# One hybrid decoder layer on one core: gate and up of the feed-forward parts with seven products of sums in half of their blocks

## The chip, the core and the metric

The kernel runs on one core of a Trainium2 chip. The metric is the device time of one execution in microseconds, lower is better. The engines are TensorE (PE, its weight loads PEld), VectorE (DVE), ScalarE (ACT), GpSimd (POOL) and SyncE (SP), which issues most loads.

## The reference

The layer takes 256 tokens of width 2048. It has two feed-forward parts (FFN) of hidden width 5632, and between them a mixing part (attention and a recurrent group) that the change doesn't touch but for the form of one update.

```python
def swiglu(h, w_gate, w_up, w_down):
    return (jax.nn.silu(h @ w_gate) * (h @ w_up)) @ w_down
...
x = x + 0.5 * swiglu(rmsnorm(x, norm_ffn1[i]), w1_gate[i], w1_up[i], w1_down[i])
...
x = x + jnp.concatenate([o_mla, o_rwkv], axis=-1) @ w_out[i]
x = x + 0.5 * swiglu(rmsnorm(x, norm_ffn2[i]), w2_gate[i], w2_up[i], w2_down[i])
```

All tensors are float32.

## The kernel before

**Products.** Every float32 product is made of three matmuls of 128x128 by 128x512: each operand is split into a part in the fp32r type and a remainder (`hi`, `lo`), and hi x hi, hi x lo and lo x hi are added up in PSUM. The tokens are two tiles of 128 (TT = 2). Their transposed form for all 16 contraction tiles lies in `xT_hi` and `xT_lo` during an FFN; `gains` are multiplied in as it is made (`turn_x` on TensorE, `xT_parts_hi` on ScalarE, `xT_parts_lo` on VectorE).

**Blocks.** Weights come in blocks of 1 MB (128 partitions x 2048 columns). Block n goes through a ring: SyncE loads it into one of three buffers of `raw` (it waits until `split_lo` of block n - 3 is done, semaphore `lo_ready`), ScalarE copies it to `whi` (`split_hi`, three buffers, may run when block n - 3 has been used), VectorE takes the difference as `wlo` (`split_lo`, two buffers, when block n - 2 has been used, `block_used`), and TensorE uses it for 24 matmuls. Each engine has its queue in program order, and semaphores are the only ties between them.

**Passes.** The hidden width is 11 pieces of 512 columns (NFF = 11). One piece takes four gate blocks, four up blocks and four down blocks. The first piece has its gate and up blocks alone; then come ten passes (`pe_columns`, `dve_columns`, and the loop in `act_ffn`), nine in a hardware loop and one outside. In pass i TensorE does gate of piece i + 1 into banks 0 and 1, turns the hidden rows of piece i (`h_turn`, eight transposes into banks 6 and 7), does up of piece i + 1 into banks 2 and 3, and the four down blocks of piece i in banks 4 to 7. Beside it ScalarE makes `silu_g`, VectorE makes `hidden` after the last up block, the low part of the turned rows (`hT_part_lo`) and `update_x`, which adds half of a down chunk of 512 columns to x in two instructions, one for each token tile. A last `down` closes the FFN. ScalarE and VectorE run one block ahead of TensorE: while TensorE uses block n, VectorE splits block n + 1, and what else it does in that stretch stands in the code under the same step s.

**First piece.** In FFN 1 the norm's sums of squares (`square_x`), its factor (`factor`, and a power on GpSimd) and the turning of x lie beside the first eight blocks.

Of the kernel before, what the change touches and what calls it, by code (L numbers as in the profile page):

```python
# [56 lines left out]
BLOCKS = GATE + 16  # L57

# [59 lines left out]
def hybrid_layer(nc, table, w, out):  # L118
    where = constant_table()[1]
    ctx = ExitStack()  # L120
    with ctx:
# [150 lines left out]
        def sem(name):  # L272
# [13 lines left out]
            sem, ("silu_ready", "h_ready", "h_turned", "hT_hi_ready", "hT_ready"))  # L286
        vec, pool_chain, zero_row = sem("vec"), sem("pool_chain"), sem("zero_row")
# [36 lines left out]
        READ_FFN1, READ_OUT, READ_FFN2 = 2, 2 + 4 * NFF, 6 + 4 * NFF  # L324
# [8 lines left out]

        def split_hi(act, n, it=0):
            if n >= BLOCKS:
                return
            wd = block_width(n)
            act.wait_ge(raw_loaded[n % RAW], 16 * (n // RAW + 1) + 64 * it)
            if n >= WHI:
                act.wait_ge(block_used, n - WHI + 1 + 12 * it)  # L340
            nc.scalar.activation(whi[:, n % WHI, 0:wd], raw[:, n % RAW, 0:wd], ACT.Copy).then_inc(hi_ready, 1)  # L341

        def split_lo(dve, n, it=0):
            if n >= BLOCKS:
                return
            wd = block_width(n)
# [23 lines left out]
        def turn_bank(k, u):  # L370

            return 4 + u if k == 2 and u < 2 else 2 + (u % 6 if k == 0 else u % 2)

        def turn_x(pe, k, units):

            for u in units:
                if k == 0 and u % 2 == 0:
                    pe.wait_ge(x_loaded[u // 2], 16)
                if k and u % 2 == 0:
                    pe.wait_ge(banks_read, (READ_FFN1 + 4 * NFF, READ_FFN2, READ_FFN2 + 4 * NFF)[k - 1] - 3 + u // 2)  # L380
                if u >= {0: 6, 2: 4}.get(k, 2):
                    pe.wait_ge(xT_ready, 8 * k + u - (1 if k else 5))
# [32 lines left out]
        def h_turn(pe, f, i, it=0, b=6):  # L415
            pe.wait_ge(h_ready, NFF * f + i + 1 + it)
            if b == 6:
                pe.wait_ge(banks_read, (READ_FFN1, READ_FFN2)[f] + 4 * i + 4 * it)
# [6 lines left out]
        def down(pe, f, n, i, it=0, last=False, turn_next=False):  # L425
            h_hi, h_lo = (last_hT_hi, last_hT_lo) if last else (hT_hi, hT_lo)
            for j in range(4):
                if turn_next and j == 2:
                    h_turn(pe, f, i + 1, b=0)
                if j == 0:  # L430
                    pe.wait_ge(hT_ready, NFF * f + i + 1 + it)
                if j >= 2 or last:
                    pe.wait_ge(banks_read, (READ_FFN1, READ_FFN2)[f] + 4 * i + j - 1 + 4 * it)
                products(pe, n + j, h_hi, h_lo, range(FKT), [(4 + 2 * (j % 2), 5 + 2 * (j % 2))], COLS, True, True, it)
# [3 lines left out]
        def first_products(pe):  # L438

            for j in range(FKT):  # L440
                pe.wait_ge(first_lo_ready if j < FKT // 2 else lo_ready, 1)
                for t in range(TT):
                    acc, c = PS[:, t, :], slice(j * COLS, (j + 1) * COLS)
                    a, b = xT_hi[:, j, t * P:(t + 1) * P], xT_lo[:, j, t * P:(t + 1) * P]
                    nc.tensor.matmul(acc, a, whi[:, 0, c], start=j == 0, stop=False)
                    nc.tensor.matmul(acc, a, wlo[:, 0, c], start=False, stop=False)
                    ins = nc.tensor.matmul(acc, b, whi[:, 0, c], start=False, stop=False)
            ins.then_inc(block_used, 1)

        def pe_columns(pe, f, n, i, it=0, turn_next=False):  # L450

            pe.wait_ge(silu_ready, NFF * f + i + 1 + it)
            for s in range(4):
                products(pe, n + s, xT_hi, xT_lo, range(4 * s, 4 * s + 4), [(0, 1)], COLS, s == 0, s == 3, it)
            h_turn(pe, f, i, it)
            for s in range(4):
                products(pe, n + 4 + s, xT_hi, xT_lo, range(4 * s, 4 * s + 4), [(2, 3)], COLS, s == 0, s == 3, it)
            down(pe, f, n + 8, i, it, turn_next=turn_next)

        def pe_ffn(pe, f, B):  # L460
            turn_x(pe, 2 * f, range(2 * f, 4))
            for s in range(4):
                pe.wait_ge(xT_ready, 16 * f + 2 * s + 2)
                if (f, s) == (0, 0):
                    first_products(pe)
                else:
                    products(pe, B + s, xT_hi, xT_lo, range(4 * s, 4 * s + 4), [(0, 1)], COLS, s == 0, s == 3)
                if s < 2:
                    turn_x(pe, 2 * f, (2 * s + 4, 2 * s + 5))
            if f == 0:  # L470
                pe.wait_ge(banks_read, 1)
                pe.wait_ge(xT_ready, 6)
                pe.wait_ge(gains_loaded, 80)
                nc.tensor.transpose(PS[:, 7, 0:70], gain_rows[:, :], ident[0:70, 0:70]).then_inc(gains_turned, 1)
            for s in range(4):
# [1595 lines left out]
```

## Time and profile before

| what | value |
|---|---|
| median of 3 runs | 2046.76 us (2046.42 to 2051.57) |
| span of the profiled execution | 2045.4 us |
| TensorE's matmuls busy | 2017.3 us, 99% |
| VectorE busy | 1142.9 us, 56% |
| ScalarE busy | 869.0 us, 42% |
| granted clock of TensorE, mean | 0.999 |

The profiled execution has no time of its own in the results; its span runs from the first to the last instruction, and the median of the runs lies 1.4 us above it. Busy times of matmuls overlap in their pipeline, so a busy TensorE isn't a TensorE at its peak. A wait in a row is put down to the engine whose semaphore came last.

### The profile page before, as it was taken

To read this page: it belongs to the slowest core of one execution; us is meant where nothing else is said; L and a number is where in the kernel's file an instruction comes from. 1 tells how busy PE (TensorE), PEld (TensorE's weight loads), DVE (VectorE), ACT (ScalarE), POOL (GpSimd) and SP (SyncE) were. 2 spreads that over 40 slices of the span, in tenths; PEclk is the share of its full clock that TensorE was granted. 3 is DMA by queue.
4 is the path that set the end of the run, shared out by engine and by line. 5 is a ranking of instruction groups with operands and counts; after the bars stand their busy time and mean duration, and the time that the engine had idled before them with its cause. 6 is when DMAs were issued, how large, how long until landed. Compare 5 with 4: busy or idle time off the path is not lost.

```text
span 2045.4 us, 27608 instructions
## 1 busy us (share of the span) xinstructions
PE 2017.3 (99%) x11416; PEld 1683.9 (82%) x11416; DVE 1142.9 (56%) x1012; ACT 869.0 (42%) x847; POOL 134.9 (7%) x110
## 2 busy tenths in 40 slices
PE   8999999999999999999998999999999999999999
PEld 6888888888888889888787888888888888888887
DVE  4455545554555464756788545545554555545564
ACT  6333333333333345854344345333333333343353
POOL 0000000000000001344433000000000000000000
PEclk9999999999999999999999999999999999999999
DMA  7565555655655556667412556555656655555554
GB/s 262 186 195 195 185 185 191 198 185 187 195 193 185 191 155 215 201 196 221 123 41 70 190 165 206 185 186 194 193 185 190 195 189 187 193 195 185 186 185 144
DMA packets 190049, 373.62 MB, mean 183 GB/s; under 512 B 7110, under 2 KB 16962, under 8 KB 189980
## 3 DMA queue, kind: packets, MB, share of 16 engines
q1 hardware_dynamic: 186300, 361.47, 54.9%
q0 software_dynamic: 3680, 11.15, 1.8%
q8 instruction: 53, 0.87, 0.2%
q14 instruction: 16, 0.13, 0.0%
HBM read 363.94 MB, written 5.52 MB: 181 GB/s over the span
## 4 chain that ended last, share of the span: by engine, by line
PE 96%; DVE 2%; issue 0%; DMA 0%; ACT 0%; SPq 0%; DVEq 0%
PE PS L364 29%; PE PS L366 29%; PE PS L365 29%; PE PS L1341 3%; PE PS L421 1%; PE PS L385 1%; PE PS L1305 0%; DMA x_resid<-in_x 0%; DVE wlo L350 0%; DVE AB L1675 0%; PE PS L1412 0%; PE PS L1323 0%; PE PS L1279 0%; DVE AK L1675 0%; PE PS L1270 0%
## 5 line engine op out<-in xcount | busy, mean ns | idle before, releaser
L350 DVE TENSOR_TENSOR wlo<-raw,whi 128x2048 fp32r<-128x2048 f32 (+1 forms) x338 | 777.5, 2301 | 759.5 <-PE PS L366 755.5
L341 ACT ACTIVATE whi<-raw 128x2048 fp32r<-128x2048 f32 (+1 forms) x338 | 643.1, 1903 | 988.9 <-PE PS L366 983.9
L364 PE MATMUL PS<-whi,xT_hi 128*128 128x512 f32 (+2 forms) x1936 | 752.6, 389 | 0.0
L366 PE MATMUL PS<-whi,xT_lo 128*128 128x512 f32 (+2 forms) x1936 | 748.0, 386 | 0.0
L365 PE MATMUL PS<-wlo,xT_hi 128*128 128x512 f32 (+2 forms) x1936 | 747.5, 386 | 0.0
L366 PEld LDWEIGHTS PS<-whi,xT_lo 128*128 128x128 f32 x1936 | 363.5, 188 | 73.4
L364 PEld LDWEIGHTS PS<-whi,xT_hi 128*128 128x128 f32 x1936 | 363.6, 188 | 72.1 <-issue 0.4
L365 PEld LDWEIGHTS PS<-wlo,xT_hi 128*128 128x128 f32 x1936 | 363.7, 188 | 71.7
L364 PE MATMUL PS<-whi,hT_hi 128*128 128x512 f32 x680 | 264.8, 389 | 0.1
L366 PE MATMUL PS<-whi,hT_lo 128*128 128x512 f32 x680 | 264.6, 389 | 0.0
L365 PE MATMUL PS<-wlo,hT_hi 128*128 128x512 f32 x680 | 264.6, 389 | 0.0
L364 PEld LDWEIGHTS PS<-whi,hT_hi 128*128 128x128 f32 x680 | 127.6, 188 | 26.8 <-issue 0.5
L366 PEld LDWEIGHTS PS<-whi,hT_lo 128*128 128x128 f32 x680 | 127.6, 188 | 26.5
L365 PEld LDWEIGHTS PS<-wlo,hT_hi 128*128 128x128 f32 x680 | 127.6, 188 | 26.4
L556 DVE SCALAR_TENSOR_TENSOR x_resid<-PS,x_resid 128x512 f32<-128x512 f32 x184 | 118.0, 682 | 51.0 <-PE PS L366 51.0
L826 POOL TENSOR_TENSOR rstd<-rstd,con 128x2 f32<-128x2 f32 x6 | 6.3, 1044 | 1610.6 <-DVE rstd L821 1610.6
L403 DVE SCALAR_TENSOR_TENSOR xT_lo<-PS,gains,xT_hi 128x256 fp32r<-128x256 f32 x64 | 26.6, 477 | 28.1 <-ACT xT_hi L394 28.0
L394 ACT ACTIVATE xT_hi<-PS,gains 128x256 fp32r<-128x256 f32 x64 | 25.3, 476 | 38.0 <-PE PS L385 33.6
L1341 PE MATMUL PS<-XT,AB 64*64 64x64 f32 x640 | 26.4, 227 | 7.5 <-DVE XT L1689 4.8
L1341 PEld LDWEIGHTS PS<-XT,AB 64*64 64x64 f32 x640 | 22.1, 139 | 12.0 <-DVE XT L1702 5.7
L541 DVE SCALAR_TENSOR_TENSOR h<-PS,rstd,silu_g 128x512 f32<-128x512 f32 x44 | 30.9, 743 | 0.0
L547 DVE TENSOR_TENSOR hT_lo<-PS,hT_hi 128x1024 fp32r<-128x1024 f32 x20 | 24.5, 1224 | 10.1 <-ACT hT_hi L490 10.1
(334 smaller groups left out, 1079.6 us busy)
## 6 DMA issues: line engine op xcount, KB each, us to landing
raw<-in_w_gate SPq DMA_DIRECT2D x88, 1024.0 KB, 5.2
raw<-in_w_up SPq DMA_DIRECT2D x88, 1024.0 KB, 5.2
raw<-in_w_down SPq DMA_DIRECT2D x88, 1024.0 KB, 5.1
raw<-in_w_in SPq DMA_DIRECT2D x28, 1024.0 KB, 5.6
raw<-in_w_out SPq DMA_DIRECT2D x16, 1024.0 KB, 5.1
raw<-in_w_ple_gate SPq DMA_DIRECT2D x16, 1024.0 KB, 5.1
raw<-in_w_q_b SPq DMA_DIRECT2D x3, 1024.0 KB, 5.5
z_scratch<-zst POOLq DMA_DIRECT2D x6, 512.0 KB, 3.2
```

What stands on the lines that cost most here:

```text
L341: nc.scalar.activation(whi[:, n % WHI, 0:wd], raw[:, n % RAW, 0:wd], ACT.Copy).then_inc(hi_ready, 1)
L350: nc.vector.tensor_tensor(wlo[:, n % WLO, 0:wd], raw[:, n % RAW, 0:wd], f32(whi[:, n % WHI, 0:wd]), ALU.subtract).then_inc(lo_ready, 1)
L364: nc.tensor.matmul(acc, a, whi[:, n % WHI, c], start=st, stop=False)
L365: nc.tensor.matmul(acc, a, wlo[:, n % WLO, c], start=False, stop=False)
L366: ins = nc.tensor.matmul(acc, b, whi[:, n % WHI, c], start=False, stop=en)
L385: ins = nc.tensor.transpose(PS[:, turn_bank(k, u), j * SEQ + t * P:j * SEQ + (t + 1) * P], x[:, t, (2 * u + j) * P:(2 * u + j + 1) * P], i ...
L394: ins = nc.scalar.activation(xT_hi[:, kt, :], PS[:, turn_bank(k, u), j * SEQ:(j + 1) * SEQ], ACT.Copy, scale=gains[:, 16 * k + kt:16 * k + ...
L403: ins = nc.vector.scalar_tensor_tensor(xT_lo[:, kt, :], PS[:, turn_bank(k, u), j * SEQ:(j + 1) * SEQ], gains[:, 16 * k + kt:16 * k + kt + ...
L541: ins = nc.vector.scalar_tensor_tensor(h[:, t, :], PS[:, 2 + t, :], rstd[:, 4 * f + t:4 * f + t + 1], silu_g[:, t, :], ALU.mult, ALU.mult)
L547: nc.vector.tensor_tensor((dst or hT_lo)[:, :, :].rearrange("p (b j) s -> p b (j s)", b=2), PS[:, b:b + 2, :], f32((hi or hT_hi)[:, :, :]) ...
L556: ins = nc.vector.scalar_tensor_tensor(x[:, t, j * COLS:(j + 1) * COLS], PS[:, b + t, :], factor, x[:, t, j * COLS:(j + 1) * COLS], ALU.mu ...
L1341: ins = nc.tensor.matmul(PS[half(c), bank, out_col:out_col + CHUNK], a[half(c), s, a_cols], b[half(c)], start=start, stop=stop)
```

## The change

Take two contraction tiles (a pair) and both token tiles as a 2 x 2 block matrix A, and the pair's rows of the up and gate weights as a 2 x 2 block matrix B. Then A x B is the up and gate contribution of that pair for both token tiles. It takes eight products of blocks, or seven products of sums and differences of blocks with more additions (Winograd's form).

- A block now holds a pair with 512 columns of up and of gate (`load_unit`, two loads of 512 KB). Eight such units replace four gate and four up blocks.
- The first piece uses eight products for all pairs. In the ten passes, units 1, 3, 5 and 7 (pairs 0 to 3) use seven products, the even ones (pairs 4 to 7) eight.
- Weight sums: `weight_forms` (three dependent VectorE instructions on 1024, 512 and 512 columns into `T`), `forms_hi` (ScalarE, 2048), `forms_lo` (VectorE, 2048 into `t_lo`). Three quarters of the raw unit are split as before (1536 columns, `first_col`).
- Token sums: once for each FFN and each of four pairs, `token_sums` and `token_lo` on VectorE and `token_hi` on ScalarE, beside blocks 4 to 7 of the first piece. They overwrite the pair's part of `xT_hi` and `xT_lo` and fill `more_hi` and `more_lo`.
- The seven sums add up in PSUM banks over the four units; then `first_sum` (ScalarE) and `combine_gate`, `combine_up` (VectorE, five instructions) form gate and up. The even units add into banks 1, 4, 6 and 7.
- All eight PSUM banks are in use by the units. A pass now starts with `h_turn` into banks 2 and 3, then has the units of piece i + 1, then the down blocks, of which chunk j uses banks 2j and 2j + 1. `h_turn` waits for the `update_x` of chunk 2 of the pass before, the third output of the first unit for that of chunk 3.
- `hidden` is made under the down blocks. In the first piece it comes straight before `h_turn`.
- `update_x` is one instruction of 1024 columns, everywhere it is used.
- x is turned one unit of two tiles at a time after each block.

The diff, cut to its core:

```diff
+        def weight_forms(dve, n, it=0):
...
+            nc.vector.tensor_tensor(T[:, 0:2, :], src[:, 1:3, :], src[:, 0:1, :].broadcast_to([P, 2, COLS]),
+                                    ALU.subtract).then_inc(t_pair, 1)
+            dve.wait_ge(t_pair, forms_of(n, it))
+            nc.vector.tensor_tensor(T[:, 2, :], T[:, 1, :], src[:, 1, :], ALU.add).then_inc(t_third, 1)
+            dve.wait_ge(t_third, forms_of(n, it))
+            nc.vector.tensor_tensor(T[:, 3, :], T[:, 2, :], src[:, 3, :], ALU.subtract).then_inc(t_ready, 1)
...
+                ins = seven_product(m, P1, False, first, last)
+                if last:
+                    ins.then_inc(p_done, 1)
+                seven_product(m, P3, False, False, last)
+                seven_product(m, P2, False, False, last)
+                pe.wait_ge(t_lo_ready, forms_of(m, it))
+                if v == 1:
+                    pe.wait_ge(hT_ready, NFF * f + i + 1 + it)
+                for product in (P6, P7, P4):
...
-        def pe_columns(pe, f, n, i, it=0, turn_next=False):
...
+        def pe_pass(pe, f, i, it=0, turn_next=False):
+            if i:
+                pe.wait_ge(x_updated, evacs(f, i - 1, 2) + 4 * it)
+            h_turn(pe, f, i, it)
+            pe_units(pe, f, i, it)
+            down(pe, f, i, it, turn_next=turn_next)
...
-            for t in range(TT):
-                ins = nc.vector.scalar_tensor_tensor(x[:, t, j * COLS:(j + 1) * COLS], PS[:, b + t, :], factor,
-                                                     x[:, t, j * COLS:(j + 1) * COLS], ALU.mult, ALU.add)
-            ins.then_inc(banks_read, 1)
+            nc.vector.scalar_tensor_tensor(x[:, :, j * COLS:(j + 1) * COLS], PS[:, banks[0]:banks[1] + 1, :], factor,
+                                           x[:, :, j * COLS:(j + 1) * COLS], ALU.mult, ALU.add).then_inc(done, 1)
...
+        def dve_pass(dve, f, i, it=0, turn_next=False):
+
+            n = FFN_BASE[f] + PAIRS + 12 * i
             for s in range(12):
+                if s == 0 and i:
+                    down_out(dve, f, i - 1, 3, it)
+                if s == 8:
+                    combine_up(dve, f, i, it)
+                split_lo(dve, n + s + 1, it)
+                if s == 0:
                     hT_part_lo(dve, f, i, it)
+                if s in (0, 2, 4, 6):
+                    forms_lo(dve, n + s + 1, it)
+                if s in (1, 3, 5) or (s == 11 and not turn_next):
+                    weight_forms(dve, n + s + 2, it)
+                if s == 7:
+                    combine_gate(dve, f, i, it)
                 if s == 8:
+                    hidden(dve, f, i, it)
                 if s >= 9:
+                    down_out(dve, f, i, s - 9, it)
...
+            for s in range(PAIRS):
+                split_lo(dve, B + s + 1)
+                if s + 2 < PAIRS:
+                    xT_parts_lo(dve, 2 * f, (s + 2,))
+                if s >= 4:
+                    token_sums(dve, f, s - 4)
+                    token_lo(dve, f, s - 4)
...
+            weight_forms(dve, B + PAIRS + 1)
+            first_hidden(dve, f, B)
+            dve_pass(dve, f, 0)
```

The order of VectorE's instructions at the end of a pass, before: the last three down blocks, in the loop.

```order
L350 TENSOR_TENSOR wlo<-raw,whi 128x2048 [waits block_used,hi_ready]
L556 SCALAR_TENSOR_TENSOR x_resid<-PS,x_resid 128x512 [waits block_used]
L556 SCALAR_TENSOR_TENSOR x_resid<-PS,x_resid 128x512
L556 SCALAR_TENSOR_TENSOR x_resid<-PS,x_resid 128x512 [waits block_used]
L556 SCALAR_TENSOR_TENSOR x_resid<-PS,x_resid 128x512
```

The same place of the change (first of the ten passes; L425 is `split_lo`, L437 to L442 `weight_forms`, L782 `update_x`).

```order
L425 TENSOR_TENSOR wlo<-raw,whi 128x2048 [waits block_used,hi_ready]
L437 TENSOR_TENSOR T<-raw 128x1024 [waits raw_loaded0,t_lo_ready]
L440 TENSOR_TENSOR T<-T,raw 128x512 [waits t_pair]
L442 TENSOR_TENSOR T<-T,raw 128x512 [waits t_third]
L782 SCALAR_TENSOR_TENSOR x_resid<-PS,x_resid 128x2x512 [waits block_used]
```

The three sums of weights stand between the split and the update of chunk 2, for which TensorE's transposes now wait.

VectorE in the first piece before, around blocks 4 to 7 of FFN 1 (L821 is the norm's factor, L597 the copy of gains, L541 `hidden`).

```order
L350 TENSOR_TENSOR wlo<-raw,whi 128x2048 [waits block_used,hi_ready] x2
L821 TENSOR_SCALAR rstd<-sums 128x2 [waits squares]
L350 TENSOR_TENSOR wlo<-raw,whi 128x2048 [waits block_used,hi_ready] x3
L597 COPY gains<-PS 128x54 [waits gains_turned]
L350 TENSOR_TENSOR wlo<-raw,whi 128x2048 [waits block_used,hi_ready] x2
L541 SCALAR_TENSOR_TENSOR h<-PS,rstd,silu_g 128x512 [waits block_used,silu_ready]
```

The change at block 5 (L504 is `xT_parts_lo`, L792 to L800 `token_sums`, L804 and L806 `token_lo`).

```order
L504 SCALAR_TENSOR_TENSOR xT_lo<-PS,gains,xT_hi 128x256 [waits xT_hi_ready]
L504 SCALAR_TENSOR_TENSOR xT_lo<-PS,gains,xT_hi 128x256
L792 TENSOR_TENSOR tok<-xT_hi,xT_lo 128x2x2x128 [waits block_used]
L796 TENSOR_SCALAR tok<-tok 128x128 [waits vec]
L797 TENSOR_TENSOR tok<-tok 128x128
L798 SCALAR_TENSOR_TENSOR tok<-tok 128x128
L799 SCALAR_TENSOR_TENSOR tok<-tok 128x128 [waits vec]
L800 TENSOR_TENSOR tok<-tok 128x128 [waits vec]
L804 TENSOR_TENSOR xT_lo<-tok,xT_hi 128x512 [waits tok_hi]
L806 TENSOR_TENSOR more_lo<-tok,more_hi 128x384
L425 TENSOR_TENSOR wlo<-raw,whi 128x2048 [waits block_used,hi_ready]
```

A token step now stands ahead of each split from block 6 on, and holds a wait for ScalarE (`tok_hi`).

## Rows read from the trace of the kernel before

**Rows 1.** The page: span, and busy time of each engine

```profile
span 2045.4 us, 27608 instructions
...
PE 2017.3 (99%) x11416; PEld 1683.9 (82%) x11416; DVE 1142.9 (56%) x1012; ACT 869.0 (42%) x847; POOL 134.9 (7%) x110
```

**Rows 2.** The page: the chain that ended last, by engine

```profile
PE 96%; DVE 2%; issue 0%; DMA 0%; ACT 0%; SPq 0%; DVEq 0%
```

**Rows 3.** The chain in order of time, a pass: start us, us, what

```profile
147.72 0.87 PE PS L421 x8
...
213.91 0.87 PE PS L421 x8
```

**Rows 4.** Timeline of ScalarE in a pass: start, length, operation [idle before]

```profile
225.73 1.92 ACT L341 ACTIVATE whi<-raw 128x2048 fp32r<-128x2048 f32 x1 [3.52 <-PE PS L366]
231.17 1.92 ACT L341 ACTIVATE whi<-raw 128x2048 fp32r<-128x2048 f32 x1 [3.52 <-PE PS L366]
```

**Rows 5.** The page: groups of VectorE; xcount | busy us, mean ns | idle

```profile
L350 DVE TENSOR_TENSOR wlo<-raw,whi 128x2048 fp32r<-128x2048 f32 (+1 forms) x338 | 777.5, 2301 | 759.5 <-PE PS L366 755.5
...
L556 DVE SCALAR_TENSOR_TENSOR x_resid<-PS,x_resid 128x512 f32<-128x512 f32 x184 | 118.0, 682 | 51.0 <-PE PS L366 51.0
...
L547 DVE TENSOR_TENSOR hT_lo<-PS,hT_hi 128x1024 fp32r<-128x1024 f32 x20 | 24.5, 1224 | 10.1 <-ACT hT_hi L490 10.1
```

**Rows 6.** Timeline of VectorE in the same pass

```profile
236.68 2.29 DVE L350 TENSOR_TENSOR wlo<-raw,whi 128x2048 fp32r<-128x2048 f32 x1 [3.15 <-PE PS L366]
238.89 1.41 DVE L541 SCALAR_TENSOR_TENSOR h<-PS,rstd,silu_g 128x512 f32<-128x512 f32 x2
```

**Rows 7.** Groups of VectorE by form, columns as in rows 5

```profile
L350 DVE TENSOR_TENSOR wlo<-raw,whi 128x1280 fp32r<-128x1280 f32 x4 | 6.0, 1493 | 11.1 <-PE PS L366 11.1
...
L1067 DVE TENSOR_TENSOR sc<-sc,den 128x1024 f32<-128x1024 f32 x2 | 4.4, 2214 | 0.1
...
L1737 DVE TENSOR_TENSOR S<-PS,pc 128x128 f32<-128x128 f32 x4 | 1.2, 290 | 1.4 <-PE PS L1430 1.4
```

**Rows 8.** Timeline of VectorE near the end: each waits for the one before

```profile
2026.85 1.22 DVE L2029 TENSOR_TENSOR gate_s<-gate_s,proj 128x1024 f32<-128x1024 f32 x1
2028.10 1.23 DVE L2030 TENSOR_TENSOR x_resid<-x_resid,gate_s 128x1024 f32<-128x1024 f32 x1
```

**Rows 9.** Timeline of VectorE and TensorE where x is turned after FFN 1

```profile
746.76 1.66 DVE L403 SCALAR_TENSOR_TENSOR xT_lo<-PS,gains,xT_hi 128x256 fp32r<-128x256 f32 x4
...
747.79 1.35 PE L385 MATMUL PS<-con,x_resid 128*128 128x128 f32 x8 [1.50 <-DVE xT_lo L403]
```

**Rows 10.** Timeline of ScalarE in the first piece

```profile
31.37 1.92 ACT L410 ACTIVATE scratch<-x_resid 128x2048 f32<-128x2048 f32 x1
...
33.41 1.92 ACT L410 ACTIVATE scratch<-x_resid 128x2048 f32<-128x2048 f32 x1
...
39.89 1.28 ACT L485 ACT_TABLE_LOAD   x1
```

**Rows 11.** Windows at the end: length, busy (count) by engine, granted clock, DMA

```profile
2042.00:2043.50 1.50, 0.00 (x0) 0.00 (x0) 1.04 (x3) 0.00 (x0) 0.00 (x0) 0.79 0.22 76
2043.50:2045.40 1.90, 0.00 (x0) 0.00 (x0) 0.00 (x0) 0.00 (x0) 0.00 (x0) 0.50 0.23 78
```

**Rows 12.** Timeline of TensorE at the start

```profile
10.73 1.97 PE L385 MATMUL PS<-con,x_resid 128*128 128x128 f32 x8 [2.15 <-DMA x_resid<-in_x]
...
12.93 0.63 PE L446 MATMUL PS<-wlo,xT_hi 128*128 128x512 f32 x1
13.35 0.63 PE L447 MATMUL PS<-whi,xT_lo 128*128 128x512 f32 x1
...
19.34 1.04 PE L385 MATMUL PS<-con,x_resid 128*128 128x128 f32 x8
```

**Rows 13.** Timeline of ScalarE as FFN 2 begins

```profile
1219.23 2.07 ACT L1976 ACTIVATE proj<-PS 128x512 f32<-128x512 f32 x4 [1.61 <-PE PS L366]
```

**Rows 14.** The page: loads, KB each, us from issue to landing

```profile
raw<-in_w_gate SPq DMA_DIRECT2D x88, 1024.0 KB, 5.2
```

More of the change, by code:

```diff
@@ L423, in h_turn, with evacs, steps, eight_products @@
             ins.then_inc(h_turned, 1)
-        def down(pe, f, n, i, it=0, last=False, turn_next=False):
+        def evacs(f, i, j):
+            return 4 * ((NFF - 1) * f + i) + j + 1
+        def steps(f, i, k):
+            return 5 * ((NFF - 1) * f + i) + k
+        OUT_11, OUT_21, OUT_12, OUT_22 = (1, 0, 1), (4, 1, 1), (6, 0, 0), (7, 1, 0)
+        def eight_products(n, out, kk, first, last):
+            bank, t, side = out
+            kt, c = 2 * pair_of(n) + kk, slice((2 * kk + side) * COLS, (2 * kk + side + 1) * COLS)
+            a, b = xT_hi[:, kt, t * P:(t + 1) * P], xT_lo[:, kt, t * P:(t + 1) * P]
+            nc.tensor.matmul(PS[:, bank, :], a, whi[:, n % WHI, c], start=first, stop=False)
+            nc.tensor.matmul(PS[:, bank, :], a, wlo[:, n % WLO, c], start=False, stop=False)
+            return nc.tensor.matmul(PS[:, bank, :], b, whi[:, n % WHI, c], start=False, stop=last)
@@ new lines, in hybrid_layer, with token_form, seven_product @@
+        P1, P2, P3, P4, P5, P6, P7 = (0, 0, 1), (1, 1, 3), (6, 6, 2), (4, 2, 3), (5, 3, 0), (2, 4, 2), (3, 5, 1)
+        def token_form(f, p):
+            if f < 4:
+                return tuple(a[:, 2 * p + f // 2, (f % 2) * P:(f % 2 + 1) * P] for a in (xT_hi, xT_lo))
+            return tuple(a[:, p, (f - 4) * P:(f - 3) * P] for a in (more_hi, more_lo))
+        def seven_product(n, product, of_sums, first, last):
+            bank, f, k = product
+            a, b = token_form(f, pair_of(n))
+            c = slice(k * COLS, (k + 1) * COLS)
+            hi, lo = (t_hi[:, k, :], t_lo[:, k, :]) if of_sums else (whi[:, n % WHI, c], wlo[:, n % WLO, c])
+            nc.tensor.matmul(PS[:, bank, :], a, hi, start=first, stop=False)
+            nc.tensor.matmul(PS[:, bank, :], a, lo, start=False, stop=False)
+            return nc.tensor.matmul(PS[:, bank, :], b, hi, start=False, stop=last)
@@ L426, in down @@
+        def down(pe, f, i, it=0, last=False, turn_next=False):
+            n = FFN_BASE[f] + PAIRS + 12 * i + (0 if last else PAIRS)
             h_hi, h_lo = (last_hT_hi, last_hT_lo) if last else (hT_hi, hT_lo)
@@ L466, in pe_ffn @@
                 else:
[L467 to L475, printed above, removed]
-                products(pe, B + 4 + s, xT_hi, xT_lo, range(4 * s, 4 * s + 4), [(2, 3)], COLS, s == 0, s == 3)
@@ L477, in pe_ffn @@
-            with pe.Fori(0, NFF - 2) as it:
-                pe_columns(pe, f, B + 8, 0, it)
-            pe_columns(pe, f, B + FFN_BLOCKS - 16, NFF - 2, turn_next=True)
-            down(pe, f, B + FFN_BLOCKS - 4, NFF - 1, last=True)
-        def silu(act, f, B, it=0):
-            act.wait_ge(block_used, B + 4 + 12 * it)
+                    pe.wait_ge(lo_ready, B + s + 1)
+                    for out in (OUT_11, OUT_21, OUT_12, OUT_22):
+                        if (f, s) == (1, 0) and out == OUT_21:
+                            pe.wait_ge(proj_evac, 2)
+                        for kk in range(2):
+                            ins = eight_products(B + s, out, kk, s == 0 and kk == 0, s == PAIRS - 1 and kk == 1)
@@ L546, in hT_part_lo, with hidden @@
+        def hidden(dve, f, i, it):
+            dve.wait_ge(combined, steps(f, i, 5) + 5 * it)
+            dve.wait_ge(silu_ready, NFF * f + i + 2 + it)
+            for t in range(TT):
+                ins = nc.vector.scalar_tensor_tensor(h[:, t, :], h[:, t, :], rstd[:, 4 * f + t:4 * f + t + 1],
+                                                     G[:, 2 * t, :], ALU.mult, ALU.mult)
+            ins.then_inc(h_ready, 1)
+        def hT_part_lo(dve, f, i, it=0, dst=None, hi=None, b=2):
             dve.wait_ge(hT_hi_ready, NFF * f + i + 1 + it)
```

398 lines of the change are left out of this document (269 added, 129 removed).

## The prediction, made before the change was run

> **What bounds the kernel now.** The page comes first: TensorE is busy for 99% of the span VectorE for 56%, ScalarE for 42% [rows 1]. Busy shares alone don't name a bound, so the chain that ended last is next: 96% of it is TensorE's [rows 2]. In the feed-forward (FFN) loops the same chain shows the eight transposes of `h_turn` at 147.72 and 213.91 us [rows 3], so one pass is 66.19 us. The timeline of ScalarE has its copies 5.44 us apart, each after 3.52 us of waiting for TensorE [rows 4]. That is one weight block of 24 products: one product each 0.2267 us. Twelve blocks (288 products) are 65.3 us, and the transposes add 0.9 us. TensorE never waits inside a pass, and the others wait for it. VectorE spends some 35 us in a pass: twelve splits at 2.3, eight `update_x` halves at 0.68, two of `hidden` and `hT_part_lo` at 1.22 [rows 5].
>
> **The gain.** A unit of two row pairs holds the same two contraction tiles for gate and for up, so its eight 128x512 products (24 matmuls) can be seven (21). Four units per pass give 12 matmuls less. The first piece of each FFN keeps eight products, ten passes use seven: 2 x 10 x 12 = 240 matmuls, 240 x 0.2267 = **54.4 us less** work on TensorE. Nothing else in TensorE's streams changes in number but the grouping of transposes. A pass is then 276 x 0.2267 + 0.9 = 63.5 us if TensorE never waits.
>
> **What VectorE gets.** Prices are from rows: 2.29 us for 2048 columns, with the next unconnected instruction starting 2.21 after (236.68 to 238.89) [rows 6]; 1.22 for 1024 [rows 5]; 0.68 for 512 [rows 5]; for 1536 the 1280 form (1.49) and 2048 give 1.76; for 128 columns 0.29 [rows 7]. An instruction that waits for the one before it starts 0.03 after that one's end [rows 8], so a dependence costs 0.11 more than none. In a pass of seven products the splits cost 8 x 2.21 + 4 x 1.68 = 24.4; the sums of weights 4 x 2.6 = 10.4 and their low parts 4 x 2.21 = 8.8; the two combinations 1.26 + 0.73 + 0.61 + 1.26 + 1.15 = 5.0; `hidden` 1.3, `hT_part_lo` 1.15, four `update_x` of 1024 at 1.15 each 4.6, about 0.1 each under the two halves before. Together 55.7 us of 63.5, 88%. It fits as an average; what counts is where it doesn't fit.
>
> **End of each pass.** In the order now, the last down block is covered on VectorE by split, `weight_forms` and `update_x` of chunk 2, and TensorE's `h_turn` of the next pass waits for that `update_x`, since it writes banks 2 and 3 and the next unit bank 4. Before, `h_turn` stood four blocks into the pass with `hidden` done long ago. From the end of down block 2: 0.11 to VectorE's start, 2.21 split, 1.22 + 0.03 + 0.69 + 0.03 + 0.61 sums, 1.22 update (nearest row: 1.22 for 1024 columns out of PSUM) = 6.12, and 0.16 to TensorE's start. This last figure is from the turn of x, where a quarter of VectorE's group of four (1.66 us from 746.76) ends the wait for 747.79: the second instruction ends near 747.63 [rows 9], since each is 0.48 long and starts 0.39 after the one before. TensorE is ready 5.44 - 0.16 = 5.28 after the same end. The wait is 1.0, and inside the loop a register instruction stands in front of the transposes and holds this wait, so I take 1.1 (bounds 0.6, if the dependences cost nothing, and 1.5). Ten passes per FFN have nine such joints: 18 x 1.1 = **19.8**. Behind the waiting transposes stands the whole next unit. VectorE's queue then holds chunk 3's update, the split, `hT_part_lo` and the low parts: 1.15 + 1.68 + 1.15 + 2.29 = 6.3 us, and they are wanted only 0.9 + 5.4 + 2.0 = 8.3 us later, behind nine matmuls of the first seven-product unit. No stall there, nor at the other three (4.8 + 5.44 us of TensorE against 2.21 + 2.6 + 1.68 + 2.29 = 8.8).
>
> **Second down block.** `combine_gate` can start when product P6 of the last unit is done, 2.9 us into it, and ends 2.8 us later; then come 1.15 + 1.26 for `combine_up` and 2.21 for the split that down block 1 needs: 2.9 + 0.1 + 2.65 + 2.4 + 2.2 = 10.25 us against 4.76 + 5.44 = 10.2 of TensorE. With the 0.16 to start this is 0.25 per pass (0 to 0.6): 20 x 0.25 = **5.0**.
>
> **First piece.** Here `token_sums` and `token_lo` are new, four times per FFN, each with a trip over ScalarE in the middle while VectorE stands. One step: 0.69, four small ones in three dependences to 1.95 from its start, 0.05 to ScalarE, 1.05 for two copies, 0.05 back, 0.61 + 0.48: 4.2 us. Behind it in VectorE's queue is the split that TensorE needs next. After block 4: transposes, `xT_parts_hi` and `_lo` to 2.2 (0.48 each instruction [rows 9]), the step to 6.45, the split to 8.74, start 8.9, while TensorE is ready at 6.2: stall **2.7**. After block 5 `square_x` stands ahead of the token copy on ScalarE: two times 2.04 us [rows 10] behind a copy of 1.92 that ends at 9.1 on this clock, so the token step ends at 15.3 and the split at 17.6, and block 7 starts at 17.7 instead of 14.35: stall **3.4**. From there VectorE has two more steps (8.4), one split (2.2), the first `weight_forms` (2.6), `hidden` (1.4) and small ones (0.3), in all 15.1 us to the first `h_turn`, against 5.6 of block 7: stall **9.5**. ScalarE's table load of 1.28 [rows 10] and the silu end before `hidden` by this sum, so they cost nothing; without that cover they would cost about 1.3 after the last token copy, up to 1. Sum 15.6 per FFN (13 to 18, by 0.1 to 0.2 us per small instruction either way), **31.2** for two. Before, `hidden` had its turn under gate products.
>
> **The clock.** After nearly 10 us without a matmul I expect TensorE at its lower level. The trace shows it at the end: with no matmul after 2042, the granted clock is 0.79 up to 2043.5 and 0.50 from there on [rows 11], that is 1.2 of 2.4 GHz. At the start, after idle time, products follow 0.42 us apart instead of 0.23, and the granted clock isn't recorded low there, but the spacing says it [rows 12]. Seven products went so, 1.4 us lost, and eight transposes took 1.97 instead of 1.03 [rows 12]: **2.4** per event, two events: 4.8 (0 to 7). The stalls of 2.7 and 3.4 may lower it too, but the block behind each then runs under VectorE's longer chain. The Trainium skill ("TensorE: Matmul & The Clock Gate", section "HAM oscillation") says that idle gaps put TensorE back to half its clock and each has to be warmed up again; by that rule the penalty is in the sum, by a clock that stays up the time would be 2050. The trace agrees at its end.
>
> **Edges.** In FFN 1 eight transposes move behind the first product: 0.9 [rows 3]; an earlier first product could give some back, I take none. In FFN 2 the third product group waits for four copies of `proj`, 2.07 us from 1219.23 [rows 13], against 1.36 us of products: 1.1. Loads: two halves of 512 KB in place of 1 MB with the same three buffers; a block lands 5.2 us after its issue [rows 14], over 4 us ahead of its use by this schedule, so nothing. The copies `first_sum` and the silu on ScalarE lie beside TensorE; ScalarE has some 35 us of work in 64. Edges: **2.0**.
>
> **Sum.** -54.4 + 19.8 + 5.0 + 31.2 + 4.8 + 2.0 = +8.4. Against the profiled execution's span 2045.4 [rows 1] that is 2053.8; the median of the runs lies 1.4 above that span, so 2046.8 + 8.4 = **2055 us**.
>
> **Rivals.** (1) No change to speak of, chance 0.31: the waits come to 48 to 60 us. Clock at full level after the gap (-4.8) alone gives 2050; joints of 0.7 instead of 1.1 (-7.2) give 2048. For it: every term is a small difference of two long sums. Against: the first-pass chain is dependent work in queue order. (2) Faster, chance 0.13: the seven products pay because the token steps don't hold TensorE. The place is the three waits before the first `h_turn`; their price with the clock is 36 us, and without any of it the time is 2019. It decides below 21.5 us for both FFNs, 10.7 each. Only the last wait alone is 9.5 by rows. (3) Much slower, within the 0.56 for slower: the first sum reads one operand repeated over two halves. A VectorE row of the attention with a repeated operand took 2.21 us for 1024 columns, not 1.22 [rows 7]. At 1.0 more per joint and 2 in the first pieces this gives 2075; other repeated operands in this trace show no such cost, so 0.05 of the 0.56. Outside this, the forecast itself holds about 0.51.
>
> **How the numbers follow.** A measurement of this kernel tells about 0.3% (6.1 us) from no change; the bound for slower is 2052.9, 2 us under my sum. With all low bounds the sum is near -20, with all high ones +29; these don't come together, and some 12 us each way hold most: 2042 to 2066. The likeliest case alone is 2050 to 2062. Faster 0.13, same 0.31, slower 0.56.
>
> **What would show it.** In the changed profile: about 240 matmuls less; period of `h_turn` 64.8 to 65.0 us; TensorE waits for VectorE's update of x at each `h_turn` near 1 us, for the split before down block 1 near 0.3; three waits near 2.7, 3.4 and 9.5 us in each first piece, and slow products after the last. The prediction is wrong if the token steps overlap better, or if dependent VectorE instructions cost other than 0.03 after an end.

## The result and the profile after

The changed kernel takes 2063.14 us (median of 4, 2062.29 to 2063.84) against 2047.13 for the kernel before: ratio 1.0076, 95% interval 1.0062 to 1.0091. It is slower, as forecast, and inside the range of 2042 to 2066, near its upper end; but the sum said +8.4 and the profiled executions differ by 2061.8 - 2045.4 = 16.4 us.

The page after the change, against [rows 1, 5] (L782 is `update_x`):

```profile
span 2061.8 us, 28682 instructions
...
PE 1990.7 (97%) x11176; PEld 1643.4 (80%) x11176; DVE 1594.0 (77%) x1404; ACT 998.1 (48%) x963; POOL 137.9 (7%) x110
...
L782 DVE SCALAR_TENSOR_TENSOR x_resid<-PS,x_resid 128x1024 f32<-128x1024 f32 x92 | 110.5, 1218 | 19.7 <-PE PS L467 19.7
```

Matmuls fell by 240, to 11176. TensorE is busy for 97% of a longer span. Now the waits of TensorE, which decide (us in total, times, longest):

```profile
PE PS L520 <- DVE h L739: 16.4, 2, 8.8
PE PS L520 <- DVE x_resid L782: 14.6, 18, 0.8
PE PS L539 <- DVE wlo L425: 9.5, 4, 3.1
...
PE PS L539 <- ACT proj L2239: 0.8, 1, 0.8
```

L520 is `h_turn`, L539 the first product of a block. All the places that the sum names are there: two first `h_turn`s, 18 joints, four blocks of the first pieces, the third product group of FFN 2. The chain in order of time gives the stages (first pass and a steady one; last `h_turn` of FFN 1; the four transposes of p behind the mixing part; the same for FFN 2), to be laid beside [rows 3]:

```profile
75.22 1.94 PE PS L520 x8
...
142.82 1.09 PE PS L520 x8
...
207.92 1.09 PE PS L520 x8
...
663.54 1.09 PE PS L520 x8
...
717.00 0.87 PE PS L520 x8
...
1179.30 0.44 PE PS L2194 x4
...
1292.06 1.94 PE PS L520 x8
...
1358.84 1.10 PE PS L520 x8
...
1932.94 0.87 PE PS L520 x8
```

And the same marks in the chain of the kernel before (L421 is its `h_turn`, four blocks into the first pass, so 21.76 us behind the end of the first piece):

```profile
81.55 0.87 PE PS L421 x8
...
710.76 0.87 PE PS L421 x8
...
1168.81 0.44 PE PS L1931 x4
...
1287.22 0.87 PE PS L421 x8
...
1916.44 0.87 PE PS L421 x8
```

| stage | before | after | difference |
|---|---|---|---|
| start to end of first piece, FFN 1 | 59.79 | 75.22 | +15.4 |
| passes to the last `h_turn` | 650.97 | 641.78 | -9.2 |
| to the transposes of p (mixing) | 458.05 | 462.30 | +4.3 |
| to end of first piece, FFN 2 | 96.65 | 112.76 | +16.1 |
| passes to the last `h_turn` | 650.98 | 640.88 | -10.1 |
| rest | 128.96 | 128.86 | -0.1 |

Two things don't stand in the sum. The steady pass is 65.10 us long, over the 64.8 to 65.0 forecast, and the mixing part, in which no line is changed, is 4.3 us longer. The experiments follow them, and test the terms.

### The profile page after: what moved, and what is told of

It reads as the page before. It is cut to its first block, busy times and chain, and to the rows that moved or that the text cites. A ratio compares the mean times of both kernels' runs of the same rounds, so it can differ in the third digit from the quotient of the medians.

```text
span 2061.8 us, 28682 instructions
## 1 busy us (share of the span) xinstructions
PE 1990.7 (97%) x11176; PEld 1643.4 (80%) x11176; DVE 1594.0 (77%) x1404; ACT 998.1 (48%) x963; POOL 137.9 (7%) x110
## 4 chain that ended last, share of the span: by engine, by line
PE 88%; DVE 6%; issue 4%; ACT 1%; DMA 0%; DVEq 0%; SPq 0%
PE PS L465 12%; PE PS L467 12%; PE PS L466 12%; PE PS L539 8%; PE PS L541 8%; PE PS L540 8%; PE PS L557 6%; PE PS L556 6%; PE PS L558 6%; PE PS L1604 2%; PE PS L520 1%; DVE T L437 1%; DVE x_resid L782 1%; DVE wlo L425 1%; DVE T L440 1%
## 5 line engine op out<-in xcount | busy, mean ns | idle before, releaser
L425 DVE TENSOR_TENSOR wlo<-raw,whi 128x2048 fp32r<-128x2048 f32 (+2 forms) x338 | 732.2, 2167 | 295.9 <-PE PS L467 211.6
L416 ACT ACTIVATE whi<-raw 128x2048 fp32r<-128x2048 f32 (+2 forms) x338 | 606.4, 1795 | 417.1 <-PE PS L467 325.7
L539 PE MATMUL PS<-whi,xT_hi 128*128 128x512 f32 x768 | 307.1, 400 | 13.6 <-DVE wlo L425 9.5
L541 PE MATMUL PS<-whi,xT_lo 128*128 128x512 f32 x768 | 302.8, 394 | 0.0
L540 PE MATMUL PS<-wlo,xT_hi 128*128 128x512 f32 x768 | 301.6, 393 | 0.0
L465 PE MATMUL PS<-whi,xT_hi 128*128 128x512 f32 (+2 forms) x536 | 206.4, 385 | 0.0
L467 PE MATMUL PS<-whi,xT_lo 128*128 128x512 f32 (+2 forms) x536 | 203.6, 380 | 0.0
L466 PE MATMUL PS<-wlo,xT_hi 128*128 128x512 f32 (+2 forms) x536 | 203.4, 379 | 0.0
L539 PEld LDWEIGHTS PS<-whi,xT_hi 128*128 128x128 f32 x768 | 146.3, 191 | 45.6 <-issue 14.3
L541 PEld LDWEIGHTS PS<-whi,xT_lo 128*128 128x128 f32 x768 | 145.8, 190 | 32.7
L540 PEld LDWEIGHTS PS<-wlo,xT_hi 128*128 128x128 f32 x768 | 146.4, 191 | 30.8
L782 DVE SCALAR_TENSOR_TENSOR x_resid<-PS,x_resid 128x1024 f32<-128x1024 f32 x92 | 110.5, 1218 | 19.7 <-PE PS L467 19.7
L1089 POOL TENSOR_TENSOR rstd<-rstd,con 128x2 f32<-128x2 f32 x6 | 10.2, 1700 | 1614.3 <-DVE rstd L1084 1614.3
```

What stands on the lines that cost most here:

```text
L416: nc.scalar.activation(whi[:, n % WHI, a:wd], raw[:, n % RAW, a:wd], ACT.Copy).then_inc(hi_ready, 1)
L425: nc.vector.tensor_tensor(wlo[:, n % WLO, a:wd], raw[:, n % RAW, a:wd], f32(whi[:, n % WHI, a:wd]), ALU.subtract).then_inc(lo_ready, 1)
L465: nc.tensor.matmul(acc, a, whi[:, n % WHI, c], start=st, stop=False)
L466: nc.tensor.matmul(acc, a, wlo[:, n % WLO, c], start=False, stop=False)
L467: ins = nc.tensor.matmul(acc, b, whi[:, n % WHI, c], start=False, stop=en)
L539: nc.tensor.matmul(PS[:, bank, :], a, whi[:, n % WHI, c], start=first, stop=False)
```

## The experiments

"The kernel before" is timed beside each; it had 2046.85 to 2047.12. Times are medians.

**e_update: the other part of the change alone**, made in the kernel before.

```
-            for t in range(TT):
-                ins = nc.vector.scalar_tensor_tensor(x[:, t, ...], PS[:, b + t, :], factor, x[:, t, ...], ...)
-            ins.then_inc(banks_read, 1)
+            nc.vector.scalar_tensor_tensor(x[:, :, ...], PS[:, b:b + 2, :], factor, x[:, :, ...], ...).then_inc(banks_read, 1)
```

> The kernel before, with one part of the change alone: x is updated by one VectorE instruction over both token tiles in place of two. My theory: VectorE's update was never waited for there, so the time stays within 2 us of the kernel before (2047); an update of 1024 columns takes 1.22 us where the two halves took 1.29 together. Rival, that this part costs or gains time by itself (the next down block is waiting for the banks): then the time moves by more than 3 us either way, since it is done 88 times.

Measured: 2047.87 us, ratio 1.0005 (0.9995 to 1.0014). No cost of this part shows (the interval runs from -1.0 to +2.9 us), so most of the loss of 16 us lies with the seven products and their order.

**e_joint: the sums of weights behind the update that is waited for.**

```
-                if s in (1, 3, 5) or (s == 11 and not turn_next):
+                if s in (1, 3, 5):
                     weight_forms(dve, n + s + 2, it)
...
                     down_out(dve, f, i, s - 9, it)
+                if s == 11 and not turn_next:
+                    weight_forms(dve, n + s + 2, it)
```

> The changed kernel, with the sums of weights for the next pass's second unit (the call of weight_forms in the twelfth step of a pass) moved behind the update of chunk 2 that h_turn waits for. My theory, that the joint is a matter of VectorE's queue order: the wait at h_turn goes and nothing takes its place, the period falls from 65.10 to 63.7 to 64.0 us, and the time by 18 times 1.1 to 1.3 us, to 2040 to 2043. Rival, that VectorE is too full for the pass (55.7 us of work by the sum in 63.5): then the stall comes back at the next wait of TensorE, for the second unit's low parts or for chunk 3, the period stays above 64.7 and the time above 2056.

Measured: 2043.79 us, 0.9984 (0.9974 to 0.9993) of the kernel before: 19.4 less than the changed kernel. First VectorE at a joint of the changed kernel, and TensorE's `h_turn` there:

```profile
266.87 2.29 DVE L425 TENSOR_TENSOR wlo<-raw,whi 128x2048 fp32r<-128x2048 f32 x1 [2.01 <-PE PS L467]
269.08 1.22 DVE L437 TENSOR_TENSOR T<-raw 128x1024 f32<-128x1024 f32 x1
270.33 0.69 DVE L440 TENSOR_TENSOR T<-T,raw 128x512 f32<-128x512 f32 x1
271.06 0.69 DVE L442 TENSOR_TENSOR T<-T,raw 128x512 f32<-128x512 f32 x1
271.67 2.35 DVE L782 SCALAR_TENSOR_TENSOR x_resid<-PS,x_resid 128x1024 f32<-128x1024 f32 x2
...
273.02 1.09 PE L520 MATMUL PS<-con,h 128*128 128x128 f32 x8 [0.82 <-DVE x_resid L782]
```

The update starts 4.80 us after the split and `h_turn` stands until its first instruction ends. After the edit the update follows the split, and the chain has the transposes 64.03 us apart, (462.63 - 206.51) / 4, at their 0.87 us:

```profile
206.51 0.87 PE PS L520 x8
...
462.63 0.87 PE PS L520 x8
```

65.10 - 64.03 = 1.07 per joint, and no new wait of TensorE in the passes. The trace shows 0.82 of idle time, counted from the end of the matmul ahead. Without a wait `h_turn` starts before that end, which the same place after the edit shows:

```profile
270.13 0.40 PE L467 MATMUL PS<-whi,hT_lo 128*128 128x512 f32 x1
270.36 1.04 PE L520 MATMUL PS<-con,h 128*128 128x128 f32 x8
```

This overlap of 0.17 us (270.13 + 0.40 - 270.36) is lost with the wait, and makes up most of the other 0.25. The rival of a full VectorE falls.

**e_first: the first piece in another order.** The core, on VectorE:

```
                 split_lo(dve, B + s + 1)
+                if 2 <= s <= 5:
+                    token_lo(dve, f, s - 2)
+                if 1 <= s <= 4:
+                    token_sums(dve, f, s - 1)
                 if s + 2 < PAIRS:
                     xT_parts_lo(dve, 2 * f, (s + 2,))
-                if s >= 4:
-                    token_sums(dve, f, s - 4)
-                    token_lo(dve, f, s - 4)
```

ScalarE has `token_hi` at s of 1 to 4, a square each at 5 and 6, VectorE has the norm's `factor` one step later, and ScalarE's first silu waits for a new semaphore behind product group OUT_21 of block 7.

> The changed kernel with the first piece of each FFN put in another order: the token step of a pair is begun after blocks 0 to 3 of the first piece instead of 4 to 7, its last part (token_lo) stands one step later so that VectorE does not wait for ScalarE's copies, the two squares stand apart, and the first silu waits for the gate products of the last block alone. The work is the same. My theory (dependent work in queue order): the three waits of 2.4, 3.1 and 8.8 us in each FFN come down to about 3.3 in all, so 22 to 25 us go for two FFNs, and some 5 us of slow clock with them if the clock stays up: 2033 to 2041. Rival, that these waits are VectorE's amount of work and not its order: under 10 us go, 2053 or more. The clock is told apart by the granted clock over the first pass: with a wait of 3 us or less it stays at 1.0, or it falls all the same, and then 5 us less are won.

Measured: 2038.27 us, 0.9958 (0.9941 to 0.9974), 24.9 less than the changed kernel with the same work: already faster than the kernel before. What the step looked like in the changed kernel, VectorE and ScalarE after block 4:

```profile
45.10 0.68 DVE L792 TENSOR_TENSOR tok<-xT_hi,xT_lo 128x512 f32<-128x512 f32 x1
...
46.80 0.29 DVE L800 TENSOR_TENSOR tok<-tok 128x128 f32<-128x128 f32 x1
47.13 0.63 ACT L685 ACTIVATE xT_hi<-tok 128x512 fp32r<-128x512 f32 x1 [1.05 <-DVE tok L800]
47.67 0.51 ACT L686 ACTIVATE more_hi<-tok 128x384 fp32r<-128x384 f32 x1
48.21 0.69 DVE L804 TENSOR_TENSOR xT_lo<-tok,xT_hi 128x512 fp32r<-128x512 f32 x1 [1.11 <-ACT more_hi L686]
48.82 0.55 DVE L806 TENSOR_TENSOR more_lo<-tok,more_hi 128x384 fp32r<-128x384 f32 x1
49.29 2.28 DVE L425 TENSOR_TENSOR wlo<-raw,whi 128x2048 fp32r<-128x2048 f32 x1
```

4.19 us from its start to the split, 1.11 of it idle, as summed (4.2). In the new order the only waits left in the first pieces were those before the first `h_turn`s, 3.0 and 3.2 us, beside the start and the 0.8 for proj. Both answers to the question about the clock came: in FFN 1 the granted clock was 0.72 over the 6 us behind the wait of 3.0 us and the first pass took 66.74 us, 1.6 over the others; in FFN 2, after 3.2 us, it stayed at 1.00 and the pass took 65.13.

**e_all: both, and the split for down block 1 ahead of `combine_up`.**

```
-                if s == 8:
-                    combine_up(dve, f, i, it)
                 split_lo(dve, n + s + 1, it)
+                if s == 8:
+                    combine_up(dve, f, i, it)
```

> Both edits of the two other runs of the changed kernel together, and in each pass the split for the second down block ahead of combine_up. My theory: the terms add up. From 2063: 18 joints of 1.1 to 1.3 (20 to 23), 20 second down blocks of 0.25 (5), first pieces 22 to 25, clock 0 to 9, so 2002 to 2016, which is 1.5 to 2.2% under the kernel before, near what 240 matmuls are worth. Rival, that the seven products lose by VectorE being the bound: then the time stays near or over the kernel before, 2040 or more.

Measured: 2015.36 us, 0.9842 (0.9826 to 0.9859), in the range's upper end. The period is now (449.26 - 193.80) / 4 = 63.87:

```profile
193.80 0.87 PE PS L520 x8
...
449.26 0.87 PE PS L520 x8
```

So the early split is worth 64.03 - 63.87 = 0.16 per pass. In the changed kernel this wait shows in TensorE's weight loads for the down blocks (us in total, times, longest), and it is gone from e_all:

```profile
PEld PS L465 <- DVE wlo L425: 4.6, 16, 0.3
```

Nothing waits in this pass any more (TensorE is busy for all of it), and still it is longer than 276 x 0.2267 + 0.87 = 63.44. The 0.43 us that are left lie in the products themselves. Three runs looked for them, the first two made in the kernel of e_all.

**e_operands: where TensorE reads.**

```
-            hi, lo = (t_hi[:, k, :], t_lo[:, k, :]) if of_sums else (whi[:, n % WHI, c], wlo[:, n % WLO, c])
+            if of_sums:
+                c = slice((k % 3) * COLS, (k % 3 + 1) * COLS)
+            hi, lo = whi[:, n % WHI, c], wlo[:, n % WLO, c]
```

> Four of the seven products of a unit read sums of weights (tiles t_hi and t_lo); here they read columns of the block's own split (whi and wlo) instead, everything else as in the kernel with both edits and the early split, so the output is not the layer's. It asks where 0.43 us of each pass come from: the pass takes 63.87 us there, and 276 products at 0.2267 and the transposes make 63.44. Theory one, that the two more tiles which TensorE reads from cost it something: the period falls to 63.4 to 63.5 and the time by 8 us. Theory two, that it lies in what the other engines do or in TensorE's own stream: the period stays within 0.1 of 63.87 and the time within 2 us of 2015.

Measured: period 63.55, so 0.32 of the 0.43 gone. The time is 2009.47 us, but from two executions that lie 6.8 us apart (2006.07 and 2012.88); the period is the evidence.

**e_small_sums: less work for the neighbours.** The slices of T, t_hi and t_lo in `weight_forms`, `forms_hi` and `forms_lo` get `0:e`:

```
+            e = COLS if n in (FFN1 + PAIRS + 1, FFN2 + PAIRS + 1) else 8
```

> The same kernel with all its instructions, but the sums of weights and their two parts are made in full for the first unit of each FFN alone; after that they cover 8 of each 512 columns, so the products of sums read old values, and the output is not the layer's. VectorE has some 17 us less to do in each pass, ScalarE 7. Theory one, that work of the neighbours on the same memories slows the products: the period falls from 63.87 to about 63.45 and the time by about 8 us. Theory two, that it lies in TensorE's own stream: no change beyond 0.1 per pass. It is also the bound for this design: what is left above 2007 is then not VectorE's sums.

Measured: 2016.31 us, period 63.87 as before, though VectorE's busy time fell from 1590.6 to 1263.8 us. So it is not contention with the sums, and in this order VectorE's 327 us of them cost TensorE nothing; the splits and updates stayed, and were not tested. In e_operands the slow groups left were mostly those of more_hi (10 of 12 in a pass took 0.69 us). What t_hi, t_lo, more_hi and more_lo have in common is where they begin: 64 bytes past a multiple of 128 in each partition, by the sizes of the tiles ahead of them; whi, wlo, xT_hi and xT_lo begin at multiples.

**e_align: the changed kernel with this alone.**

```
+        base[0] += -base[0] % 128
         R0 = base[0]
```

> The changed kernel, nothing moved in any engine's order: all tiles from G on (t_hi, t_lo, more_hi, more_lo, h among them) lie 64 bytes further in each partition, so that they begin at multiples of 128 bytes, as whi, wlo, xT_hi and xT_lo do. Now they begin 64 bytes past one. Theory one, from the run in which products of sums read whi and wlo and the pass fell by 0.32 us with the products of more_hi still 0.69 us in three: TensorE reads slower from a place that is not a multiple of 128 bytes; then the period of h_turn falls from 65.10 by up to 0.43 us (65.10 less 0.35 to 0.45), 20 passes give 7 to 9 us, and the time is 2054 to 2056. Theory two, that it is the values or the distance of the tiles from the others: no change beyond 1 us, 2062 to 2064.

Measured: 2056.80 us, 6.3 under the changed kernel's 2063.14, and 1.0053 (1.0038 to 1.0068) of the kernel before; period (660.76 - 142.62) / 8 = 64.77, 0.33 less. Theory one holds, though both figures are a little short of it. The trace says why: this kernel still has the split for down block 1 in its old place, and the same wait for it has grown from 4.6 us:

```profile
PEld PS L466 <- DVE wlo L426: 6.0, 16, 0.4
```

These 1.4 us more are 0.07 for each of the 20 passes, which is what 0.33 lacks to the 0.40 found below where nothing waits.

Products at the end of a seven-product unit, TensorE's timeline, the first matmul of three successive groups, before the edit:

```profile
228.06 0.40 PE L556 MATMUL PS<-t_hi,xT_hi 128*128 128x512 f32 x1
...
228.76 0.39 PE L556 MATMUL PS<-t_hi,xT_hi 128*128 128x512 f32 x1
...
229.46 0.39 PE L539 MATMUL PS<-whi,xT_hi 128*128 128x512 f32 x1
```

and after it:

```profile
227.38 0.39 PE L557 MATMUL PS<-t_hi,xT_hi 128*128 128x512 f32 x1
...
228.06 0.39 PE L557 MATMUL PS<-t_hi,xT_hi 128*128 128x512 f32 x1
...
228.74 0.39 PE L540 MATMUL PS<-whi,xT_hi 128*128 128x512 f32 x1
```

A group of three matmuls took 0.70 us and now takes 0.68. The next block's first groups took 0.69 (229.46 to 230.15), though these read well-placed tiles in both, and are at 0.68 too.

**e_again: the changed kernel once more.**

> The changed kernel once more, for the clock in the mixing part. In its first profile the granted clock fell to 0.75 for some 10 us near 1125 us, and about 4 of the 16 us that the change lost lie there, though nothing of it stands there. Theory one, chance of the moment: in a second execution the clock falls elsewhere or not at all, and the last x-turn of the mixing part stands nearer 8 than 10 us behind the kernel before. Theory two, it belongs to this program's order in time: the same place and the same loss within 0.5 us, and the time within 1 us of 2063.

Measured: 2064.02 us. The second theory: the mixing part had 462.6 us against 462.3, with the clock low in the same place. The windows of the first and of the second execution (length, busy by engine, granted clock, DMA):

```profile
1100.00:1140.00 40.00, 35.18 (x626) 30.66 (x627) 29.19 (x63) 13.36 (x26) 12.21 (x8) 0.87 0.29 92
```

```profile
1100.00:1140.00 40.00, 34.78 (x624) 30.19 (x625) 29.38 (x64) 13.37 (x26) 12.20 (x8) 0.87 0.28 89
```

In its four stretches of 10 us the granted clock was 0.83, 1.00, 0.75 and 0.91 in the first execution, and 0.83, 1.00, 0.78 and 0.88 in the second; in the kernel before it was 1.00 from 1070 to 1130 us. The loss lies there too: from the last `h_turn` to the last products with `lora_t` in the chain (1080.23, before 1074.66) the changed kernel took 363.2 us against 363.9, and from there to the transposes of p 99.1 against 94.2.

But it is no property of the seven products alone: in the profile of e_update, all eight products, the same stretch took 1174.48 - 710.22 = 464.3 us, in an execution with a span of 2051.0 where the nine others had 2045.4 to 2047.5, and its granted clock fell to 0.67 and 0.78 between 1000 and 1020. In the profiles of all versions of the changed kernel the stretch took 461.0 to 464.2, with falls at several places.

**e_best, e_best2, e_best3: the rest of the wait before the first `h_turn`**, in the kernel of e_all. First on ScalarE and by token tile (the squares one block earlier, a small silu to load the table, the silu before the split), of which the part on VectorE is:

```
             for t in range(TT):
+                if t:
+                    dve.wait_ge(block_used, B + PAIRS)
+                else:
+                    dve.wait_ge(first_gate, 2 * f + 2)
```

> The kernel with both edits and the early split, and what is left of the wait ahead of the first h_turn (3.0 us in each FFN) taken down: the squares stand one block earlier, a small silu behind them brings ScalarE's table load into idle time, the first silu stands ahead of the next split, and hidden's first token tile starts when its three product groups of the last block are done and not at the end of the block. My theory: hidden's second tile alone stands behind the block, 0.7 us and the hand-overs, so the wait falls from 3.0 to 0.9 to 1.2 us, the clock stays up (1.6 us in FFN 1), and the time falls by 4 to 6 us to 2009 to 2011. Rival, that the wait has another last cause, VectorE's weight_forms or the squares: the wait stays above 2.5 us and the time within 1 us of 2015.

Measured: 2017.42 us, the waits 3.3 and 3.4: no gain. The rival had it, and the timeline of ScalarE and VectorE names the cause:

```profile
57.62 1.27 ACT L664 ACTIVATE G<-PS,rstd 128x512 f32<-128x512 f32 x2 [0.53 <-PE PS L541]
...
59.46 1.22 DVE L437 TENSOR_TENSOR T<-raw 128x1024 f32<-128x1024 f32 x1
...
61.44 0.69 DVE L442 TENSOR_TENSOR T<-T,raw 128x512 f32<-128x512 f32 x1
62.04 1.40 DVE L750 SCALAR_TENSOR_TENSOR h<-PS,rstd,G 128x512 f32<-128x512 f32 x2
```

The silu is done at 58.9, `hidden` waits behind `weight_forms`, the same fault as at the joint. So:

```
-            weight_forms(dve, B + PAIRS + 1)
             first_hidden(dve, f, B)
+            weight_forms(dve, B + PAIRS + 1)
```

> As the last best kernel, and hidden of the first piece ahead of the sums of weights for the first unit, which stood before it on VectorE and kept it back by 2.6 us. My theory: the wait at the first h_turn falls from 3.3 to 1.2 to 1.5 us in each FFN, and TensorE's clock stays up after it (there it fell in both FFNs, h_turn 1.94 us and the first pass 1.4 to 1.6 over the others): 2 times 2 and some 5 for the clock, so 2008 to 2011. Rival: the low parts of the first unit's sums are now too late and the wait comes back inside the first unit: the time stays above 2014.

Measured: 2009.83 us, both waits 0.9. With the tiles in place as in e_align:

> The same kernel with the tiles at multiples of 128 bytes. If the place is what costs TensorE, the period is 63.4 to 63.5 and the time another 8 to 9 us less, 2000 to 2003, 2.2% under the kernel before; if not, it is that of the kernel without it.

Measured: 2001.50 us (1999.58 to 2003.63), **0.9777 (0.9764 to 0.9790) of the kernel before**, and the pass, (633.38 - 125.66) / 8 = 63.47 us, is the sum of its products:

```profile
125.66 0.88 PE PS L521 x8
...
633.38 0.87 PE PS L521 x8
```

## Why the prediction came out as it did

**The gain**, -54.4: right. 240 matmuls are gone and a pass without waits takes 63.47 us in e_best3, against the 63.5 of the prediction.

**End of each pass**, 18 x 1.1: right in place, cause and size, 1.07 by e_joint, 19.3 in all. That no stall comes at the next unit was right too.

**Second down block**, 5.0: right in place, over in size. 0.16 per pass, 3.2. Part of this is a slip: the prediction's own terms, 10.25 - 10.2 + 0.16, give 0.21 and not 0.25.

**First piece** and edges, 31.2 + 2.0: measured 15.4 + 16.1 = 31.5. The waits before two blocks and `h_turn` were 5.4 and 7.6 in FFN 1, 4.0 and 8.8 in FFN 2, 25.8 together, against 2.7 + 3.4 and 9.5 twice, 31.2; the wait for proj was 0.8 for 1.1. So the waits were over-sized by 5.4 us. (A slip is in them: the terms ahead of the last wait add to 14.9 and not 15.1, which gives 9.3.) The stages lost nearly what was summed all the same, since TensorE ran partly slow between the waits, earlier than the prediction had it, and a block that ends later waits less behind. That the totals agree, 31.5 against 33.2, is luck in part: two errors of opposite sign. For proj, 2.07 - 1.36 is 0.7; the 1.1 of the sum holds 0.4 that it doesn't source. Windows over FFN 1's first piece and its end, the third figure from the end is the granted clock:

```profile
62.00:75.00 13.00, 5.65 (x22) 4.27 (x20) 10.58 (x20) 6.01 (x8) 2.69 (x1) 0.76 0.45 156
75.00:82.00 7.00, 6.78 (x23) 5.80 (x24) 4.91 (x4) 4.62 (x3) 0.00 (x0) 0.60 0.47 150
82.00:90.00 8.00, 8.00 (x36) 6.56 (x36) 5.92 (x6) 2.00 (x2) 0.00 (x0) 1.00 0.26 77
```

**The clock**, 4.8: the first passes took 67.60 and 66.78 against 65.10, so 4.2. That TensorE comes back at its lower level after the gap, 1.2 of 2.4 GHz, shows in `h_turn`'s 1.94 us and the granted clock of 0.60 around it. The Trainium skill's rule ("TensorE: Matmul & The Clock Gate", section "HAM oscillation"), that idle gaps cost a new warming up, agrees with this trace and with that of e_best. A gap need not be near 10 us: after 3.3 and 3.4 (e_best) both `h_turn`s took 1.94, after 3.0 and 3.1 (e_all) 1.06, with 1.6 us lost in the pass behind in FFN 1 (granted clock 0.72 from 64 to 70 us) and none in FFN 2 (1.00), after 0.9 (e_best2) none.

**What failed is the pricing of a product.** The step "Pass = 276 x 0.2267 + 0.9" took the time of one product from tiles that lie at multiples of 128 bytes; the change adds tiles that don't, and the products were on average 0.2283. That is 63.87 - 63.47 = 0.40 per pass, 8.0 over 20: e_align shows the cause on the changed kernel (-6.3, with 0.07 per pass gone into the longer wait for the split), e_best3 against e_best2 where nothing waits (-8.3). The forecast of the period, 64.8 to 65.0, missed 65.10 by this; without the smaller down block it would have missed by more.

**What the sum had no term for** is the mixing part, +4.3, a lower granted clock while the small matmuls run. It is measured and not explained. That it goes with the program's course in time fits e_again, a single execution; why nearly all executions of the kernel before are spared stays open.

Together: -54.4 + 19.3 + 3.2 + 8.0 + 31.5 + 4.2 + 4.3 = 16.1, of 16.4. Without the two costs that the prediction didn't have, 8.0 and 4.3, the measured terms add to +3.8. That would be 2051 us, below the 2052.9 from which the prediction calls a result slower. So the waits and their causes were right, but that the kernel is clearly slower was luck: it rests on costs that nobody forecast.

**The rivals.** (1) No change: not so, the interval's lower end is 1.0062. (2) The token steps don't hold TensorE: not in this order. It was right that they would decide it: with them reordered (e_first) the time is 0.4% under the kernel before. (3) The repeated operand: refuted, the first sum took 1.22 us for 1024 columns. The price of a dependence held as well: the next sum started at 270.33, 0.03 after the end of the first (269.08 + 1.22). Why the attention's row [rows 7] is slow was not tried.

## What to carry to other kernels

Fewer products pay only if what feeds them is queued by due time: here 54 us, as much as was saved, were lost where an instruction that TensorE waited for stood behind sums needed much later, or across a round trip to another engine, on a VectorE that was 77% busy. Moving and splitting calls, at the same work on TensorE, turned +0.8% into -1.8% (e_best2). When tiles are added, look at where in the partition they begin: a matmul's price read from other tiles doesn't hold for a badly placed one.

## What the runs showed of the hardware that was not expected

Tiles read by TensorE that begin 64 bytes past a multiple of 128 made groups of three 128x512 matmuls take 0.69 to 0.70 us in place of 0.68, in part of their groups and in groups right behind them, 0.40 us of 63.87 in a pass. Only a shift by 64 bytes was tried, so which multiple is wanted stays open. Taking 327 us of work from VectorE and 130 from ScalarE beside it made no difference (e_small_sums).
